# Finishing the prompt tokens in ranked tiles beside the last expert steps of a grouped top-2 MoE

## The reference, cut to what matters

```python
def route(x, router_w, router_bias):            # 16 experts in 4 groups, 2 chosen of one group
    s = sigmoid(x @ router_w); sb = s + router_bias
    ...
    w = s * sel                                  # sel: the two chosen experts
    return w / sum(w)

def moe_block(x, ...):
    comb = route(x, router_w, router_bias)
    hh = silu(x @ w1[e]) * (x @ w3[e]) * comb[e] # for each expert e, D_EXPERT = 256
    return sum_e hh @ w2[e]

x = layer_norm(ALPHA * x + moe_block(x), ln2_g, ln2_b)   # y_prompt, y_sample
```

## Time and profile before

| | us |
|---|---|
| median of 3 runs | 1378.2 |
| profiled execution, its own time | 1378.48 |
| its span | 1376.6 |
| TensorE busy | 1263.5 (92%) |
| VectorE busy | 736.0 (53%) |
| ScalarE busy | 413.7 (30%) |
| GpSimd busy | 178.9 (13%) |

### The profile page before, as it was taken

The page is one execution under the profiler, slowest core; times in us unless marked ns, Lnnn a source line. Parts: engine busy times, 40 slices in busy tenths (PEclk is TensorE's granted clock), DMA queues, the critical chain, the costliest instruction groups (busy, mean ns, idle before and its releaser), DMA issues.

```text
span 1376.6 us, 19619 instructions
## 1 busy us (share of the span) xinstructions
PE 1263.5 (92%) x6900; PEld 756.1 (55%) x6900; DVE 736.0 (53%) x1731; ACT 413.7 (30%) x881; POOL 178.9 (13%) x212
## 2 busy tenths in 40 slices
PE   6899999999999999889899999999649999999966
PEld 3587787777877546656666665444223333333322
DVE  6834574765745102487778764335643433334339
ACT  4322432422422101346575762213201101111016
POOL 0121031030211000210000000000010222211131
PEclk9999999999999999989999999999859999999988
DMA  9821030130201303225010006300376959495856
GB/s 298 270 70 32 18 77 0 33 61 18 73 5 48 105 7 62 80 47 151 14 41 1 17 30 187 125 31 31 142 261 205 358 199 321 128 359 153 274 188 220
DMA packets 126648, 163.19 MB, mean 119 GB/s; under 512 B 32021, under 2 KB 100933, under 8 KB 126570
## 3 DMA queue, kind: packets, MB, share of 16 engines
q1 hardware_dynamic: 112122, 112.50, 26.7%
q0 software_dynamic: 14448, 49.66, 10.5%
HBM read 225.02 MB, written 36.45 MB: 190 GB/s over the span
## 4 chain that ended last, share of the span: by engine, by line
PE 76%; DVE 15%; issue 3%; DMA 3%; ACT 2%; POOL 1%; DVEq 0%; ACTq 0%; POOLq 0%
PE act L689 16%; PE vec L1237 11%; PE vec L997 9%; PE vec L718 7%; PE vec L747 4%; PE act L922 4%; PE vec L910 3%; PE act L1250 2%; PE vec L1250 2%; PE act L934 2%; DMA arena<-x_rows,arena 2%; PE act L947 1%; DVE arena L1931 1%; PE vec L699 1%; DVE arena L1947 1%
## 5 line engine op out<-in xcount | busy, mean ns | idle before, releaser
L689 PE MATMUL act<-arena 128*128 128x352 f32 x768 | 240.3, 469 | 5.5 <-issue 4.6
L689 PEld LDWEIGHTS act<-arena 128*128 128x128 f32 x768 | 145.7, 193 | 82.7 <-issue 9.3
L1237 PE MATMUL vec<-arena 128*64 128x512 f32 x768 | 173.4, 604 | 2.6 <-issue 2.6
L997 PE MATMUL vec<-arena 128*128 128x512 f32 (+1 forms) x288 | 126.6, 594 | 0.8 <-DVE arena L1956 0.8
L1237 PEld LDWEIGHTS vec<-arena 128*64 128x64 f32 x768 | 54.4, 138 | 104.8 <-issue 104.5
L718 PE MATMUL vec<-arena 128*128 128x512 f32 (+1 forms) x256 | 100.3, 546 | 0.0
L2244 DVE TENSOR_SCALAR arena<-arena 128x256 f32<-128x256 f32 x24 | 7.1, 296 | 171.7 <-ACT arena L1585 171.7
L997 PEld LDWEIGHTS vec<-arena 128*128 128x128 f32 (+1 forms) x288 | 50.9, 180 | 68.1 <-issue 66.1
L1494 ACT ACTIVATE arena<-arena 128x640 f32<-128x640 f32 (+15 forms) x128 | 81.3, 639 | 8.7 <-DVE arena L1931 8.3
L1931 DVE CUSTOM_DVE_ANT_0 arena<-vec,arena 128x128 f32<-128x128 f32 (+6 forms) x168 | 69.0, 430 | 23.1 <-PE vec L910 16.0
L1485 ACT COPY arena<-act 128x512 f32<-128x512 f32 (+11 forms) x176 | 63.2, 429 | 54.5 <-PE act L922 54.2
(11 more groups left out here) (386 smaller groups left out, 1943.2 us busy)
## 6 DMA issues: line engine op xcount, KB each, us to landing
arena<-in_exp_w SPq DMA_DIRECT2D x144, 1024.0 KB
y_rows<-arena POOLq DMA_DIRECT2D x48, 256.0 KB, 5.0
arena<-in_w_in SPq DMA_DIRECT2D x16, 512.0 KB, 6.5
arena<-in_x_prompt SPq DMA_DIRECT2D x8, 512.0 KB, 5.7
x_spill<-arena POOLq DMA_DIRECT2D x8, 512.0 KB, 5.4
arena<-x_spill SPq DMA_DIRECT2D x8, 512.0 KB, 5.2
arena<-in_cache_fox_kv SPq DMA_DIRECT2D x16, 256.0 KB, 3.5
x_rows<-arena POOLq DMA_DIRECT2D x8, 512.0 KB, 2.9
```

What stands on the lines that cost most here:

```text
L689: last = mm(bk[:, 0:n], W[k % 2][:, c, m * P:(m + 1) * P], xT[:, c, a:a + n], start=c == 0, stop=c == NC - 1)
L997: last = mm(bk[:r], src, Wo[half][:, c, :], start=c == 0, stop=c == NC - 1)
L1237: last = mm(gu_bank[p][o], xgT[p][:, c, o], Wgu[:, slot, c, :], start=c == 0, stop=c == NC - 1)
```

## The change

A token can be finished once both of its rows are stored, so once the step of its later row is over. The change ranks the 1024 prompt tokens by that step, cuts the ranking into eight ordered tiles of 128, and takes it that ordered tile n is complete when FIRST + n = 17 + n steps are stored. It finishes tiles 0 to 4 inside steps 19 to 23 and the other four (5 to 7, and the sample tile 8) after them.

- **Ranking.** VectorE works out for each row the step it is in (`turn`), the later of the two for each token (`last_turn`), and a one-hot table by step with its running count (`in_turn`, `upto`, `before_it`). TensorE sums these over partitions (three small matmuls); VectorE turns the sums into a place for each token (`places`, after the second copy of turned rows), and one-hot matrices `in_place` and `ordered`; eight small matmuls permute token number, the two slots and the two weights into ranked order; VectorE copies the result into `order_int` and `order_c`.
- **Address in `y_rows`.** Rows of step k now lie together, so `store` is one DMA of 128 rows.
- **GpSimd's queue.** The diagonals are gone. From step 18 on it gathers the two rows of an ordered tile into two 128x1024 buffers (`pair`, two sets that alternate for tiles 0 to 6, and the token buffers for tiles 7 and 8). From step 20 on it first writes the finished tile n - 2 by index to the prompt output (`scatter`) and waits until that has landed, because the buffer is used again.
- **VectorE alone does a tile** (`finish`): weigh first row, add weighed second row, statistics, centre and scale, reciprocal, last multiply-add, all on 1024 columns from SBUF. For tiles 6 to 8 ScalarE weighs the first row. ScalarE takes the square root (`deviation`). TensorE has no part in it.
- **SP** stores only the sample output.
- On VectorE and ScalarE steps 19 to 22 are written out instead of standing in a loop.

```diff
+FIRST = 17
+    pair = [[X[:, 4 + 2 * (n % 2) + m, :] if n < 7 else X[:, 2 * (n - 7) + m, :] for m in range(2)] for n in range(NT)]
 # SP
-        for t in range(NT):
-            e.wait_ge(*E.at(("y normalised", t)))
-            e.dma_start(yp[t * P:(t + 1) * P] if t < 8 else ys, X[:rows(t), t, :]).then_inc(*E.moved("y_out"))
+        e.wait_ge(*E.at(("y normalised", 8)))
+        e.dma_start(O_["y_sample"].rearrange("b t d -> (b t) d"), pair[8][1][:NS]).then_inc(*E.moved("y_out"))
 # TensorE
+        e.wait_ge(*E.at("turns counted"))
+        mm(order_bank[:, 0:n], C["before"], in_turn...); mm(order_bank[:, 0:n], ones, before_it...)
+        mm(order_bank[:, n:n + TILES], ones, upto[:, :, 7], start=True, stop=True).then_inc(*E.done("turns summed"))
...
         gate_up(0, 0, 0)
+        e.wait_ge(*E.at("places known"))
+        for t in range(8):
+            last = mm(order_bank[:, 256:296], in_place[:, t, :], ordered[:, t].rearrange("p v n -> p (v n)"), start=t == 0, stop=t == 7)
+        last.then_inc(*E.done("order known"))
-        E.stage("combine")
-                for n in range(2):
-                    last = mm(bk[:r], weigh[:r, n, t, 0:r], gathered[:r, 2 * (t % 4) + n, o], start=n == 0, stop=n == 1)
 # ScalarE
+        def deviation(n):
+            r = P if n < 8 else NS
+            e.wait_ge(*E.at(("variance", "ln2", n)))
+            act(rstd[:r, n:n + 1], mv[:r, n, 1:2], ACT.Sqrt, bias=eps_out[:r]).then_inc(*E.done(("deviation", n)))
...
                 hidden_turned(k - 1, b)
+                if isinstance(k, int) and k >= FIRST + 2:
+                    deviation(k - FIRST - 2)
                 gate_exp(k, 1 - b)
 # VectorE
+        step(stt(turn, tile_of, 2.0, over_turn, ALU.mult, ALU.add))
+        step(tt(last_turn, turn[:, 0:8], turn[:, NT:NT + 8], ALU.max))
+        step(tt(in_turn, C["iota"][:, 0:TILES]..., last_turn..., ALU.is_equal))
+        step(e.tensor_tensor_scan(upto..., marks, in_turn..., 0.0, ALU.mult, ALU.add))
+        step(tt(before_it, upto, in_turn, ALU.subtract), "turns counted")
...
+        def finish(n):
+            e.wait_ge(*E.at(("gathered", n)))
+            if n < 6:
+                step(ts(a, a, c[:, 0], None, ALU.mult))
+            else:
+                e.wait_ge(*E.at(("first weighed", n)))
+            step(stt(b, b, c[:, 1], a, ALU.mult, ALU.add))
+            for half in range(2):
+                e.bn_stats(stats[:r, n, 6 * half:6 * half + 6], b[:, 512 * half:512 * half + 512]).then_inc(*E.done())
+            e.wait_ge(*E.own())
+            step(e.bn_aggr(mv[:r, n, :], stats[:r, n, :]), ("variance", "ln2", n))
+            step(stt(b, b, mv[:r, n, 0:1], ln_g[:r], ALU.subtract, ALU.mult))
+            e.wait_ge(*E.at(("deviation", n)))
+            step(e.reciprocal(rstd[:r, n:n + 1], rstd[:r, n:n + 1]))
+            step(stt(b, b, rstd[:r, n:n + 1], ln_b[:r], ALU.mult, ALU.add), ("y normalised", n))
...
                 rows_turned(k + 1, b)
+                if isinstance(k, int) and k >= FIRST + 2:
+                    finish(k - FIRST - 2)
                 silu(k, 1 - b)
                 output(k - 1, b, 2 * odd + b)
 # GpSimd
         def store(k):
-            for g in range(2):
-                at = HR * ((2 * g + k % 2) * SEG + k // 2)
-                e.dma_start(y_rows[at:at + HR]..., ysb[k % 2][HR * g:HR * g + HR]).then_inc(msem[f"y{k % 2}_stored"], 16)
+            e.dma_start(y_rows[k * P:(k + 1) * P]..., ysb[k % 2]).then_inc(msem[f"y{k % 2}_stored"], 16)
...
                 fetch(k + 2)
+            if k >= FIRST + 3:
+                scatter(k - FIRST - 3)
+            if k == FIRST + 1:
+                e.wait_ge(*E.at("order ready"))
+            if k >= FIRST + 1:
+                stored(k - 2)
+                if k >= FIRST + 3:
+                    e.wait_ge(*E.at(("rows out", k - FIRST - 3)))
+                gather(k - FIRST - 1, P, order_int[:, 1:3])
             if k:
                 store(k - 1)
-            if 3 <= k < 3 + NT:
-                for n in range(2):
-                    e.tensor_scalar(weigh[:, n, k - 3, :], ident, c12[:, n, k - 3:k - 2], None, ALU.mult)
+        scatter(TILES - FIRST - 3)
         store(TILES - 1)
+        e.wait_ge(*E.at(("rows out", TILES - FIRST - 3)))
+        stored(TILES - 2)
+        gather(TILES - FIRST - 1, P, order_int[:, 1:3])
+        stored(TILES - 1)
+        gather(TILES - FIRST, P, order_int[:, 1:3])
+        gather(NT - 1, NS, s_int)
+        for n in range(TILES - FIRST - 2, NT - 1):
+            scatter(n)
```

More of the change, by code:

```diff
@@ L367, in program @@
     xg = [X[:, n, :].rearrange("p (c n) -> p c n", c=NC) for n in range(4)]
-    weigh = zx.take(2 * NT * P, 2, NT)
+    in_turn, before_it, upto = (zx.take(TILES * 8, TILES) for _ in range(3))
+    in_place, ordered = zx.take(8 * P, 8), zx.take(8 * 40, 8, 5)
+    marks = ordered.rearrange("p t v n -> p (t v n)")[:, 0:TILES * 8]
+    turn_slot = zx.take(2 * NT)
+    turn, over_turn, totals, starts = zx.take(2 * NT), zx.take(2 * NT), zx.take(TILES), zx.take(TILES)
+    last_turn, place, place_tile, place_row = (zx.take(8) for _ in range(4))
+    place_int, tile8_int, row8_int = (zx.take(8, dt=I32) for _ in range(3))
+    order_int, order_c = zx.take(24, 3, dt=I32), zx.take(16, 2)
     assert zx.at <= attention_end + NC * D + 824
@@ L649, in _ @@
         next_down(SEG - 1, 1)
-        yp, ys = O_["y_prompt"][0], O_["y_sample"].rearrange("b t d -> (b t) d")
-        for t in range(NT):
-            e.wait_ge(*E.at(("y normalised", t)))
-            e.dma_start(yp[t * P:(t + 1) * P] if t < 8 else ys, X[:rows(t), t, :]).then_inc(*E.moved("y_out"))
+        e.wait_ge(*E.at(("y normalised", 8)))
+        e.dma_start(O_["y_sample"].rearrange("b t d -> (b t) d"), pair[8][1][:NS]).then_inc(*E.moved("y_out"))
+        for n in range(5, 8):
+            e.wait_ge(*E.at(("rows out", n)))
         e.wait_ge(*E.at("y_out"))
@@ L1599, in two_tiles @@
                 hidden_turned(k - 1, b)
+                if isinstance(k, int) and k >= FIRST + 2:
+                    deviation(k - FIRST - 2)
                 gate_exp(k, 1 - b)
         two_tiles(0)
-        with e.Fori(1, TILES // 2 - 1) as i:
+        with e.Fori(1, FIRST // 2 + 1) as i:
+            two_tiles(i)
+        for i in range(FIRST // 2 + 1, TILES // 2 - 1):
             two_tiles(i)
         hidden_turned(TILES - 2, 0)
+        deviation(TILES - FIRST - 3)
         gate_exp(TILES - 1, 1)
         hidden_turned(TILES - 1, 1)
-        for t in range(NT):
-            rstd_of("ln2", t)
+        for n in range(TILES - FIRST - 2, NT):
+            if n >= 6:
+                r, scale = (P, order_c[:, 0, n:n + 1]) if n < 8 else (NS, c12[:NS, 0, n:n + 1])
+                e.wait_ge(*E.at(("gathered", n)))
+                act(pair[n][0][:r], pair[n][0][:r], ACT.Copy, scale=scale).then_inc(*E.done(("first weighed", n)))
+            deviation(n)
     @block.vector
@@ L2260, in _ @@
         rows_turned(0, 0)
         rows_turned(1, 1)
+        places()
         silu(0, 0)
+        e.wait_ge(*E.at("order known"))
+        step(cp(order_int, order_bank[:, 256:280].rearrange("p (v n) -> p v n", v=3)))
+        step(cp(order_c, order_bank[:, 280:296].rearrange("p (v n) -> p v n", v=2)), "order ready")
         def two_tiles(i, odd):
@@ L2270, in _ @@
         two_tiles(0, False)
-        with e.Fori(0, TILES // 4 - 1) as i:
+        with e.Fori(0, FIRST // 4) as i:
             two_tiles(2 * i + 1, True)
             two_tiles(2 * i + 2, False)
+        for i in range(FIRST // 2 + 1, TILES // 2 - 1):
+            two_tiles(i, i % 2 == 1)
+        finish(TILES - FIRST - 3)
         silu(TILES - 1, 1)
@@ L2276, in _ @@
         output(TILES - 1, 1, 3)
[L2278 to L2304, removed]
+        for n in range(TILES - FIRST - 2, NT):
+            finish(n)
     @block.gpsimd
```

86 lines of the change are left out of this document (61 added, 25 removed).

## The result

The changed kernel takes 1365.5 us in the median of ten executions, beside 1377.2 before (also ten; the first three of them gave 1378.2). One of the ten ran in a slower state of the chip (1845.9 us at a granted clock of 0.647) and is left out of the ratio; the other nine lie between 1361.1 and 1373.1. The ratio is 0.992, interval 0.989 to 0.994, so the change is faster, by under 1%. The gain is a little over half of what the prediction forecast (1356.7). The time is inside its range for eight in ten (1348 to 1368), though not in the forecast's own (1351 to 1363).

What follows compares the result with a forecast made beforehand. TensorE's expert chain (92% busy) bounds the kernel, with 58.4 us behind the last expert. Loop +7.2, tail -28.1, early -0.7 sum to -21.6: profiled 1378.48 to 1356.9, given as 1356.7; eight-in-ten range 1348 to 1368, forecast's own 1351 to 1363.

Steps and rivals of the forecast that it cites:

- VectorE's 6.45 us hide in a step: Expert steps: finishing a tile costs VectorE 6.45, fitting between 0.6 and 7.5 behind gate-up's start if gathered rows are there.
- Rows of tiles 0 and 1 are there: Steps 19 and 20: gathers queued about 2.7 behind gate-up starts 18 and 19, a step ahead, no scatter in front.
- the prediction's own signs of being wrong: Loss already in steps 19 and 20, a wait in the first two expert steps, or gathers waiting on stores, not scatters.
- A scatter lands in 5.1 us, 8.1 beside the weight burst: GpSimd's queue, rounds 20 and 21: quiet gather's 5.1 taken for scatter(0); 8.1 for gather pairs and scatter(1) meeting full engines.
- T(22) is set by the weights, 3.9 us late: Start of gate-up 22: 1.5 MB added at 383 GB/s delays weights 3.9, to 1295.2, later than VectorE's 1294.3.
- Step 22 14.3 us, step 23 no further loss: Gate-up 22 starts 1295.2, gate-up 23 1309.5; tile 4 then ends with step 23's exp at 1316.95; loop loses 7.2.
- Rival B, the clock: TensorE waits of 4 us before gate-ups 22 and 23 drop its clock; costs 8, time 1365; chance 0.11.
- Rival A: Expert loop: transfers find room, weights are not pushed, only the tail changes; span 1347.7, time 1349.3; chance 0.16.
- Rival C: Scatters to scattered output rows are slow; landing after 12 us eats the whole gain of 21.6; chance 0.05.
- The tail: Behind the last expert output: 58.4 falls to 30.3, a gain of 28.1, VectorE last after waiting 4.2 for tile 6's pair.
- Early margins: Before the experts' first SiLU: ranking (4 us) and placement (6.6) fit VectorE's idle 6.99 and 7.97; cost 0, else 1.5.
- The 0.7 for the removed spreading: Steps 3 to 11: GpSimd no longer spreads weights and issues one store, so fetches leave earlier; credited 0.7.

Runs made afterwards that it cites:

- the version without traffic: Changed kernel without scatters and gathers of ordered tiles 0 to 4; gate-up 19 to last expert output 63.6 us (before 63.3, changed 79.6).
- finish later: Changed kernel with three sets of row buffers and each ordered tile finished one step later; gate-up 19 to last output 68.8 us, ratio to before 0.988.
- the last version: Three buffer sets, finishing one step later, TensorE sums for tiles 5 to 8, plus tile 6's rows in a free weight slot; median 1358.7 us, ratio 0.984.

## Why the prediction was right or wrong

- *VectorE's 6.45 us hide in a step.* Right. Tile 0 runs from 1253.01 to 1259.48, 6.47, and the version without traffic loses 0.3 us in five tiles.
- *Rows of tiles 0 and 1 are there.* Right for 0, wrong for 1: 1.95 late. The pair was put at T(19) + 2.7; the first issue began at T(19) + 4.8, behind a gap that has no named releaser:

```profile
1257.27 1.52 POOL L2456 DMA_INDIRECT arena<-y_rows,arena  x1 [1.35 <-issue]
```

  The store of step 17 was issued at 1253.04 and landed at 1256.24, and the gather waits for it (`stored(k - 2)`). The sum had no term for this wait. Two of the prediction's own signs of being wrong so came true in small: a gather waited on a store, and step 20 already lost 1.0 us.
- *A scatter lands in 5.1 us, 8.1 beside the weight burst.* The term of the sum that was mis-sized. Measured: 8.4, 10.2, 9.0, and 4.3 and 3.5 only from step 23 on. I took the quiet price where the engines had been quiet before, although the kernel itself now filled them: share 1.00 and 1.05 from 1264 to 1295. Each late microsecond goes round GpSimd's queue as described, to tile, SiLU and next step. The 9.0 us by which the loop was missed (16.2 for 7.2) are 1.0 in step 20, 2.3 in step 21, 0.2 in step 22 and 5.5 in step 23.
- *T(22) is set by the weights, 3.9 us late.* The place was right (step 21 loses most), the last wait was not: hidden rows came last, by 5.15 behind a wait of 1.83 for fetched rows (expected: 4.1, from 1289.8 to 1293.9, and less than the weights). With VectorE's wait taken out (finish later) the weights are late by 5.08, against 1.22 + 3.9 = 5.1 predicted. This step of the sum holds as a price; it was overtaken.
- *Step 22 14.3 us, step 23 no further loss.* Step 22 took 14.5. Step 23 lost 5.5: tile 4's rows 3.0 late, and the lower clock in turning and down, 3.68 + 2.53 for 1.94 + 1.74.
- *Rival B, the clock.* Not a case apart but a part of the case: 1.7 in gate-up 22 and 2.5 in the last down, 4.2 of the 9.0 us by which the loop was missed. I had given it 0.11 as an alternative and nothing in the sum. The argument against it was a misreading: TensorE did not idle 3.5 us before 1301.86. The chain of waits runs there over ScalarE and VectorE, while TensorE did the down matmuls:

```profile
1298.16 1.92 PE L1250 MATMUL act<-arena 128*64 128x512 f32 x8
1299.88 1.92 PE L1250 MATMUL vec<-arena 128*64 128x512 f32 x8
...
1039.95 8.79 PE L1237 MATMUL vec<-arena 128*64 128x512 f32 x32
```

  The last line is gate-up 1 of the same trace, behind a real wait of 2.50: the granted clock is 1.00 from 1036 to 1039.6 and 0.58 from 1040 to 1043. So the trace before already showed a wait of this size followed by a gate-up 1.7 longer.
- *Rival A*, no loss in the loop, is refuted: every version with transfers in it takes 68.8 or more for the stretch, not 63.3. *Rival C* came half way: scatters of 9 us, where 12 was the point of no gain.
- *The tail.* 32.2 for 30.3. Tile 6 waited 3.3 (4.2 expected), three tiles took 17.1 as worked out, and VectorE ended 26.7 behind the last output for 27.8; the miss is the 3.0 us at the close. The prediction had VectorE last there and the last scatter inside. The scatter did land inside, at 1357.6, but the end follows GpSimd's last issue by 9.0 us, and this issue itself took 1.87 in place of the 1.0 put down for it. Nothing in the trace before spoke of this, since GpSimd was done 24 us early there.
- *Early margins.* Right: no wait of TensorE grew. The 0.7 for the removed spreading was not found (from T(2) to T(19) both take 201.5), 1.7 came from the clock instead.

Still open: what GpSimd does in the 9 us behind its last issue, and how the late weights and late fetch share the 7.6 us, since both move together.

## What to carry to other kernels

Work moved into an engine's idle time brings its transfers with it, and these go into the engines' busiest stretch: price them at the full-engine latency of the trace, and again for the kernel's own fetches. A wait placed in a shared in-order queue costs what stands behind it; when it is removed, look for the next one under it, as the store under the scatter here. When the moved work is late by some microseconds, add the clock that TensorE loses in the wait, and before arguing from an idle stretch look at TensorE's own timeline: the chain of waits leaves out what an engine does beside it. When work on an engine's queue moves to the very end of a program, look at the distance from its last issue to the end of the span, not only at the landing.

## What the runs showed of the hardware

- **GpSimd's issues nearly double beside certain VectorE work.** The issue of an indirect DMA mostly takes 0.94 to 1.00 us. In the changed kernel, while VectorE finishes tiles:

```profile
1254.18 1.74 POOL L2440 DMA_INDIRECT arena<-x_rows,arena  x1 [0.30 <-issue]
```

This fetch and the last scatter (1353.38, above) both stand beside 1024-column steps with two inputs in SBUF. In the last version VectorE reads its sums from PSUM, and the scatters at 1343.67 and 1348.20 take 0.96, while the one at 1334.59, beside a step on SBUF alone, takes 1.95. The Trainium skill, SBUF — State Buffer (section SBUF: two separate sides), names VectorE operations with two SBUF inputs, beside the two-port mode, as holders of the shared ports, but these only against a GpSimd operation that reads SBUF; the prediction had weighed only the two-port step. The rows above fit this if issuing an indirect DMA counts as such a read, which no run here shows. Not all rows fit: the gather issued at 1317.87 takes 0.98 although it overlaps such a step (L2339) for 0.80 us.
- **The end of the program follows GpSimd's last issue by 8.96 us when that comes late** (nine executions with 50 indirect DMAs, 8.96 or 8.97; 8.56 with 45, 7.74 with 35). With the last issue 20 us early the close is 2.4 behind VectorE in place of 5.5.
- **Eight small matmuls in a gap of 2.5 us kept the granted clock at its upper level**: gate-up 1 took 7.10 us, not 8.79, in the one execution with them alone and in all twelve with the ordering matmuls.
